# Both expert tables streamed for two latent chunks: scattered and one-hot weights, and a first part of the products kept in DRAM

## The reference

```python
def peer(h, w_q, sub_keys, u_tab, v_tab):
    ...
    def chunk(x):                                      # 128 tokens
        q = (x @ w_q).reshape(PEER_CHUNK, PEER_HEADS, 2, PK_HALF)
        s = jnp.einsum('chpd,hpnd->chpn', q, sub_keys).astype(jnp.float32)
        st, it = lax.top_k(s, PEER_TOPK)
        ...
        best, pos = lax.top_k(cand, PEER_TOPK)
        eidx = jnp.take_along_axis(cidx, pos, axis=-1)  # 8 heads x 16 experts per token
        g = jax.nn.softmax(best, axis=-1)
        act = jax.nn.gelu(jnp.einsum('chkd,cd->chk', u_tab[eidx], x).astype(jnp.float32))
        return jnp.einsum('chk,chkd->cd', (g * act).astype(x.dtype), v_tab[eidx])
```

## Time and profile before

| | us |
|---|---|
| median of 3 runs (2457.07 to 2461.68) | 2457.78 |
| profiled execution, first to last instruction | 2458.3 |
| last score matmul of phase 1 (L986) ends | 1118.95 |
| walk over the `v` table (L1064), first to last | about 1617 to 2065 |

### The profile page before, as it was taken

One profiled execution on the slowest core, in us unless ns is written; L12 is line 12 of the kernel. 1 busy time (PEld: TensorE's weight loads), 2 busy tenths in 40 slices (PEclk: granted clock), 3 DMA queues, 4 the chain that ended last, 5 costly groups with the idle time before them and its releaser, 6 DMA issues.

```text
span 2458.3 us, 20346 instructions
## 1 busy us (share of the span) xinstructions
PE 1778.0 (72%) x6013; PEld 1073.5 (44%) x6013; DVE 1873.6 (76%) x3933; ACT 514.3 (21%) x1283; POOL 1037.4 (42%) x1028
## 2 busy tenths in 40 slices
PE   7799889889887989891334666689999996000185
PEld 3578744444356438451012333556666664000032
DVE  2451588756789466889999999888687987999955
ACT  0563116440024000110004655710000000000111
POOL 0000000115534342443774776334344446777674
PEclk9899999899999999996566877899999998555599
DMA  9785772349955695866998999589999999999997
GB/s 279 250 274 193 233 231 87 113 135 319 353 182 180 215 330 177 288 250 211 384 410 285 390 411 404 200 300 411 414 411 414 411 411 411 410 408 406 364 404 304
DMA packets 296873, 753.43 MB, mean 306 GB/s; under 512 B 21502, under 2 KB 141102, under 8 KB 296244
## 3 DMA queue, kind: packets, MB, share of 16 engines
q0 software_dynamic: 147456, 536.94, 57.3%
q1 hardware_dynamic: 149308, 215.20, 25.0%
HBM read 740.72 MB, written 11.33 MB: 306 GB/s over the span
## 4 chain that ended last, share of the span: by engine, by line
DVE 37%; PE 29%; DMA 16%; POOL 8%; issue 6%; ACT 2%; DVEq 0%; SPq 0%; ACTq 0%; POOLq 0%
PE bank L788 12%; PE pair L788 6%; DVE big L1552 5%; DVE attn L1552 4%; DMA ring_more<-in_peer_u_dram,eidx 4%; DMA attn<-in_peer_u_dram,eidx 4%; DVE work L1552 3%; PE bank L971 3%; POOL work L2118 2%; DVE ring_more L1552 2%; POOL attn L2118 2%; PE bank L761 2%; POOL big L2118 2%; DMA attn<-in_peer_v_dram,eidx 2%; PE bank L1019 1%
## 5 line engine op out<-in xcount | busy, mean ns | idle before, releaser
L1019 PE MATMUL bank<-big,work 128*128 128x512 f32 x176 | 110.6, 767 | 369.4 <-ACT work L1091 266.3
L788 PE MATMUL pair<-big 128*128 128x128 f32 (+1 forms) x1280 | 361.8, 440 | 9.1 <-DVEq L1421 6.2
L2118 POOL DMA_INDIRECT h_all<-in_peer_u_dram,eidx x109 | 122.0, 1119 | 577.9 <-DVEq L1987 352.6
L788 PE MATMUL bank<-big 128*128 128x512 f32 (+1 forms) x1056 | 310.9, 453 | 34.4 <-DVEq L1421 22.7
L1064 PE MATMUL bank<-h_all,big 128*128 128x512 f32 x608 | 266.8, 595 | 4.6 <-DMA h_all<-in_peer_v_dram 4.6
L788 PEld LDWEIGHTS pair<-big 128*128 128x128 f32 x1280 | 197.3, 194 | 160.9 <-issue 158.6
L788 PEld LDWEIGHTS bank<-big 128*128 128x128 f32 x1056 | 169.2, 199 | 172.4 <-issue 165.0
L2118 POOL DMA_INDIRECT attn<-in_peer_u_dram,eidx x166 | 163.1, 983 | 165.5 <-DVE dots L1552 97.9
L1019 PEld LDWEIGHTS bank<-big,work 128*128 128x128 f32 x176 | 38.1, 235 | 427.0 <-issue 394.9
L1552 DVE CUSTOM_DVE_ANT_0 attn<-attn,pair 128x1024 f32<-128x1024 f32 x166 | 199.5, 1219 | 25.3 <-DMA attn<-in_peer_u_dram,eidx 23.0
L1064 PEld LDWEIGHTS bank<-h_all,big 128*128 128x128 f32 x608 | 180.5, 297 | 86.7 <-DMA h_all<-in_peer_v_dram 5.4
(11 more groups left out here) (311 smaller groups left out, 3172.7 us busy)
## 6 DMA issues: line engine op xcount, KB each, us to landing
big<-in_w_in_dram SPq DMA_DIRECT2D x44, 1024.0 KB, 6.5
h_all<-in_peer_v_dram SPq DMA_DIRECT2D x76, 512.0 KB, 6.8
big<-in_w_ada_dram SPq DMA_DIRECT2D x24, 1024.0 KB, 8.1
big<-in_peer_w_q_dram SPq DMA_DIRECT2D x16, 1024.0 KB, 5.6
gf_row<-in_peer_v_dram SPq DMA_DIRECT2D x26, 512.0 KB, 6.8
work<-in_peer_v_dram SPq DMA_DIRECT2D x26, 512.0 KB, 6.8
big<-in_w_rnn_o_dram SPq DMA_DIRECT2D x8, 1024.0 KB, 7.9
big<-in_w_attn_o_dram SPq DMA_DIRECT2D x8, 1024.0 KB, 6.4
```

The costliest lines, as they stand in the source:

```text
L788: last = nc.tensor.matmul(u[:, 0:n], w[:, k, col:col + P], src[:, k, 0:n], start=(k == 0), stop=(k == KD - 1))
L1019: last = nc.tensor.matmul(psum[i][:, :], diag[:, (n - 1) % DIAGS, :], ring[r][:, i * 512:(i + 1) * 512], start=(k == first_by_tensor[c]), ...
L2118: g.indirect_dma_start(dst, None, ins["peer_" + table][0], bass.IndirectOffsetOnAxis(ap=eidx[:, c, k:k + 1], axis=0)).then_inc(landed, 16)
```

## The change

For chunks 1 and 2 the rows of `u` go too. Both tables are streamed, block by block (128 blocks of 128 experts).

- For a block of `u`, PE transposes the tile (`turn_u`, 8 transposes), ACT copies the result (`move_u`), PE multiplies it with the 256 tokens of both chunks (`products`, 8 matmuls of 256 columns), ACT takes the gelu of it (`gelu`).
- The first 34 blocks (`AHEAD_U`) of this are done before any `v` block; their results go to DRAM (`g_later`, 0.131 MB each) and come back. The others run 4 blocks (`LAG`) ahead of the `v` block.
- DVE multiplies the products with the weights of the block (`weigh`, two 128 x 128 operations, one per chunk), and PE multiplies that with the `v` tile (`sums`, four matmuls of 512 columns, as before).
- Chunk 1's weights are scattered by POOL into a matrix in DRAM (`w_flat`, 8.4 MB, 128 indirect DMAs of 128 elements, each adding; `scatter`), which 16 DMAs have filled with zeros early in phase 0. A block of it (0.066 MB) is loaded with each block. Chunk 2's weights are built by one-hots as before (32 builds, now made and scaled on DVE), beside blocks 22 to 32 of `u`; three quarters stay in SBUF.
- Chunk 2's routing moves into and right behind the score loop. Rows are now only those of chunks 0, 3 and 4, all on DVE: 560 behind the loop instead of 772 (of which 100 are multiplied by PE). The ring has 9 buffers: 6 are open first, 8 from turn `C3_ROUTED`, 9 from `C4_ROUTED`.
- DVE's order from there is made by a planner: each row counts 1.3 us, each part of a route 1.8 to 5.3 us, and a `weigh` is put in when the sum reaches its due time (`spent`, `sums_at`). ACT's answers (softmax, gelu of dots, roots) are placed by the same clock (`ask`).
- The loop of phase 1 ends without PE and ACT waiting for DVE.

```diff
-    RING = 29
+    RING = 9
...
+    AHEAD_U, LAG, KEPT, U_BUFS, V_BUFS, W_BUFS, M_BUFS = 34, 4, 8, 2, 4, 3, 2
...
+        return [0, 1, 2, 3, 4, 5] + [6, 7] * (turn >= C3_ROUTED) + [8] * (turn >= C4_ROUTED)
...
+            def turn_u(n):
...
+                for k in range(KD):
+                    last = nc.tensor.transpose(uT_ps(n)[k // 4][:, (k % 4) * P:(k % 4 + 1) * P],
+                                               u_tile[n % U_BUFS][:, k * P:(k + 1) * P], ident[:, :])
...
+            def products(n):
...
+                for k in range(KD):
+                    last = nc.tensor.matmul(a_ps[n % 2], uT_of(n)[:, k, :], featT[:, k, 0:TOKENS], start=(k == 0), stop=(k == KD - 1))
...
+            def sums(n):
+
+                pe.wait_ge(m_ready, n + 1)
+                pe.wait_ge(v_in[n % V_BUFS], 16 * (n // V_BUFS + 1))
...
+            for n in range(AHEAD_U):
+                if n + 1 < AHEAD_U:
+                    turn_u(n + 1)
+                products(n)
+                if n == IDS_AT:
+                    turn_ids()
+                for m in builds_after.get(n, ()):
+                    weights(m)
             for n in range(NKEY):
...
+                if AHEAD_U <= n + LAG < NKEY:
+                    turn_u(n + LAG)
+                sums(n)
+                if AHEAD_U <= n + LAG < NKEY:
+                    products(n + LAG)
...
+            PART_US, ROW_US, HOT_US = (1.8, 1.8, 1.8, 1.8, 4.3, 5.3, 2.8), 1.3, 1.45
+            BOTH_US, SUM_US = 8.2, 3.5
...
+                V.tensor_tensor(m[:, 0:P], g_[:, 0:P], w_first[n % W_BUFS], ALU.mult)
+                V.tensor_tensor(m[:, P:2 * P], g_[:, P:2 * P], w_second[:, n // QI % 3, :, n % QI], ALU.mult).then_inc(m_ready, 1)
...
+            def spent(us):
+
+                clock[0] += us
+                while made[0] < NKEY and clock[0] >= ALONE_US + (WORK - ALONE_US) * sums_at(made[0]) / sums_at(NKEY):
+                    weigh(made[0])
+                    made[0] += 1
...
+            for z in range(ZEROS):
+                g.dma_start(w_zero[z], zero).then_inc(zero_in, 16)
...
+            def scatter(h):
+
+                if h % 2 == 0:
+                    pool.wait_ge(pair_ready, h // 2 + 1)
+                if h:
+                    pool.wait_ge(scattered, 16 * TOPK * h)
+                for k in range(h * TOPK, (h + 1) * TOPK):
+                    g.indirect_dma_start(w_flat, bass.IndirectOffsetOnAxis(ap=widx[:, k:k + 1], axis=0),
+                                         gw[:, C1, k:k + 1], None, compute_op=ALU.add).then_inc(scattered, 16)
...
+            rows(0, BESIDE)
+            pool.wait_ge(zero_in, 16 * ZEROS)
+            for h in range(PH):
+                scatter(h)
+            rows(BESIDE, len(turns))
```

More of the change, by code:

```diff
@@ new lines, in hybrid_step @@
+        w_zero = w_flat.rearrange("(z p x) o -> z p (x o)", p=P, x=D)
+        w_block = w_flat.rearrange("(a p x) o -> a p (x o)", p=P, x=P)
+        g_later = nc.dram_tensor("g_later", (AHEAD_U, P, TOKENS), F32, kind="Internal").ap()
+        w_later = nc.dram_tensor("w_later", (P, QI * P), F32, kind="Internal").ap()
+        zero = h2_all[:, NCH - 1, :]
+        widx = eidx[:, C1, :]
+        tok = sb("tok", [P, 1])
+        iota128 = vcols
+        u_tile, v_tile = [wk(6, 2), wk(8, 2)], [wk(2, 2)] + [h2_all[:, i, :] for i in range(3)]
@@ L715, in _ @@
+            for i in range(1, NCH):
                 store(i)
@@ L1409, in _ @@
+            pe.drain().then_inc(sums_full, 1)
+        asks = {}
         @block.vector
@@ L1711, in topk, with settle @@
                 link(V.max_index(ti[:, 8:16], tv[:, 8:16], cut_))
-            def route(c, pair, between):
-                for i in range(4):
-                    hp = 4 * pair + i
-                    topk(c - C1, hp, late2[:, hp, :] if c == C1 + 1 else late34[:, c - C1 - 2, hp, :])
-                    between(i)
+            def settle(c, pair, between):
                 h = 2 * pair
@@ L1729, in route, with pair_ids, search_second @@
                 between(6)
+            def route(c, pair, between):
+                for i in range(4):
+                    hp = 4 * pair + i
+                    topk(c - C1, hp, late34[:, c - C1 - 2, hp, :])
+                    between(i)
+                settle(c, pair, between)
+            def pair_ids(c, pair):
+                h = 2 * pair
+                places_of_64(c, h)
+                for s in range(2):
+                    expert_side(h, h + 2, s)
+                if c == C1:
+                    pair_places(c, pair)
+            def search_second(hp):
+                u = (1, "sc", hp)
+                dve.wait_ge(bank_free[bank[u]], use[u])
+                topk(1, hp, late2[:, hp, :])
             dve.wait_ge(x_in, 16)
@@ new lines, in spent, with rows_beside, beside, between @@
+            def spent(us):
[3 more added lines that the diff above has]
+                    made[0] += 1
+            def rows_beside(n):
+                for _ in range(n):
+                    rows(1)
+                    spent(ROW_US)
+            def beside(n_rows):
+                def between(i):
+                    spent(PART_US[i])
+                    rows_beside(share(n_rows, i, PARTS))
+                return between
@@ new lines, in _, with hots_beside, between @@
+            next_hot = [0]
+            def hots_beside(pair):
+                def between(i):
+                    spent(PART_US[i])
+                    end = BUILDS * max(PARTS * pair + i - 1, 0) // (2 * PARTS - 2)
+                    for m in range(next_hot[0], end):
+                        one_hots(m)
+                        spent(HOT_US)
+                    next_hot[0] = end
+                return between
+            pair_ids(C1, PAIRS - 1)
+            for pair in range(PAIRS):
+                best_of_64(C1 + 1, 2 * pair)
+                before[0] += 5.0
+                pair_diffs(C1 + 1, pair)
+                pair_ids(C1 + 1, pair)
+                before[0] += 7.0
+                pair_weights(*((C1 + 1, pair - 1) if pair else (C1, PAIRS - 1)))
@@ L2094, in _ @@
+            route(C3, 3, beside(SPREAD))
+            routed(C3)
+            for pair in range(PAIRS):
+                if pair == PAIRS - 1:
+                    dve.wait_ge(final_in, 48)
+                    final(0, wk(4, 2))
+                route(C4, pair, beside(SPREAD // 2))
+            rows_beside(U4 - next_turn[0])
+            dve.wait_ge(row_used, U4)
+            gelu_dots(C3)
             routed(C4)
-            rows(step_start[4] - next_turn[0])
-            step_end(C4)
-            rows(ALONE)
```

1140 lines of the change are left out of this document (541 added, 599 removed).

## The result

The changed kernel takes 2506.6 us (median of 4, 2503.1 to 2508.0), the kernel before beside it 2459.4 us (median of 4): a ratio of 1.0188, 95% interval 1.0173 to 1.0203. It is slower by 47 us where 16 us less was forecast (2442 for 2458). The profiled execution has a span of 2501.3 us, 59 more than the 2442 of the sum.

A forecast was written before the change was run, and what follows sets the result against it. Behind the score loop, mostly DMA megabytes were taken as the bound. PE's stream from 1124, first part to 1325, walk from 1339 to 2393, end at 2412, plus 30 for queues: 2442 us, 8-in-10 range 2398 to 2530.

The forecast's parts named there:

- the scatter: On POOL behind the score loop: 215 us from about 1066, ending near 1280, ahead of the rows, so nothing counted.
- what the walk loses: Queue losses of DMA over the 1054 us walk over v: bounds 18 and 84 us, 30 taken.
- the zeros: Zero fill of 8.4 MB ahead of phase 1: bounds 0 and 20 us, 5 taken.
- three signs of being wrong: Long stretch's DMA rate under 390 GB/s, PE waiting for tiles, or the walk starting later than 1355.
- What is to be had: Behind the score loop: 452 MB for 498, the 46 MB less worth 112 us at 411 GB/s.
- The score loop: DVE falls some 13 us behind PE but catches up; PE starts on the u stream at 1124.
- The first 34 blocks: PE's u blocks at 4.33 us each, 148 us with the first turn, plus 53 for builds, ending at 1325.
- the rival of a slow PE: First 34 blocks of u at 1.2 GHz: 148 + 34 us more, about 2620; chance 0.03.
- the rival of the late scatter: From 1.6 us per scatter, rows and w_flat blocks wait; at 2.0 us each, 2488 in all; chance 0.12.
- The walk: Walk over v from 1339, longest engine sum per stretch: 136, 187, 677 and 54, together 1054 us, before queue losses.
- The last eight blocks: Blocks 120 to 127: 16 us of rows, 9 of chunk 4's sums and norm, 29 of PE: 54 us.
- The queues lose 8%: Six buffers and three engines near their limit in blocks 32 to 55 cost 84 us: 2496; chance 0.22.

The follow-up runs named there:

- the four edits: Changed kernel with zeros spread, last weigh earlier, ACT's answers one block earlier, and six gathers ahead of the scatter with small blocks ahead of V tiles 1 to 3: 2439.4 us.
- ask_early: Changed kernel with ACT answering DVE's five late requests one block of u earlier: 2489.7 us.
- combo_beside: The four edits together, with 44 instead of 32 rows used inside the score loop: 2458.5 us.
- before_again: The kernel before, unedited, run again to have its profile from the same set: 2537.1 us.

## Why the prediction was wrong, step by step

Faster was forecast, and it came out slower. The step that failed is the one that counted nothing for the scatter: the way from the last one-hots to the first `weigh` took 23 us more than the sum had. Two more terms were of the right kind and too small: what the walk loses (64 us for 30) and the zeros (13 for 5). Of the three signs of being wrong that were set, one came: the walk starts at 1365, later than 1355. The long stretch ran at 397 GB/s on average and not under 390, and PE never waited for a tile in it.

**The bytes: right.** 453 MB behind the score loop for 452, and a full rate of 404 to 411 behind 1620 against 399 to 407 now. "What is to be had" stands as a sum of bytes (45 MB, 110 us for 112); with the four edits the kernel ends up 21 us under the kernel before.

**The zeros: taken as 5 us within 0 to 20, measured 13.** The step read that there was room in DMA's share at 150 to 200 us. But the zeros go at 56 to 64, in one burst of 8.4 MB, and PE's tiles had to share the DMA engines with it (410 GB/s from 64 to 72 us, while PE waited). The window to read was that one. Spread out, they cost nothing that can be seen.

**The score loop: right**, pace and hand-over, but for 3.2 us at the hand-over.

**The first 34 blocks: right.** 4.33 us a block, and the whole stretch with its builds 194 us for 201. PE's clock is at 0.98 to 1.00 (the level of 2.4 GHz) from 1124 to 1300 with 8 transposes among 24 records, so the rival of a slow PE is out. The Trainium skill, "TensorE: Matmul & The Clock Gate", "Part 4: PE-mode transpose", says that transposes don't count as busy in the same way; the trace shows the clock at full speed in this mix all the same. DMA moved 119 to 129 GB/s up to 1300 for 140.

**The scatter: this step failed.** It took 1.24 us each, from a gather, and "so I count nothing". A scatter takes 1.55 us on POOL with 0.30 to the next, and 17 us went for landings, 265 us in all for the 215 of the sum: the rival of the late scatter, whose decision point was 1.6 us each. It also began 14 us late (1079.8 for 1066), when POOL had waited 20 us for DVE; so it ended at 1344.5, 64 us behind the 1280 of the sum. POOL's row of this run gives what it should have been:

```profile
L2206 POOL DMA_INDIRECT w_flat<-gw,eidx x128: 1537/1545/2269, 1079.8 to 1342.9; - x128
```

The price of the gather was read as the whole distance between two, 0.94 and 0.30 us, and taken as the lower bound for the scatter; then the forecast stood on that bound, although 7 us stood at the other end. The sentence on read-modify-write below 512 B in the Trainium skill, "DMA: Bandwidth & Descriptors", "Specifications", had spoken for more; that this is where the 0.6 us come from is not shown by any run. The lateness cost DVE 19 us, but the run without scatter got back only 9: the other half of the term is the wait for a small block that stands behind the scatter, issued at the same moment as V tiles and nine rows, which the sum had at nothing.

**The walk: +34 of 1084, at the sizes of three terms.** By stretches: blocks 0 to 31 took 152 for 136, 32 to 55 209 for 187, 56 to 119 698 for 677, and 120 to 127 59 for 54; so 64 us where 30 were laid aside. The bounds of 18 and 84 held it. The prediction put these losses down to the ring, and the runs show another cause for much of them: 17 us (or more) go with two waits for an answer of ACT, which one line takes away. The prediction knew of seven such waits and left them "within these bounds". The ring was not what lost most of it in the long stretch: with nine buffers DMA is full there (share 1.01), and three buffers fewer cost 21 in the whole. Whether more than six would have helped in the first 144 rows, no run tells.

In the first blocks there is a wait that neither the sum nor an edit took up. DVE waits 19 us for blocks of `g_later`, all of it by 1518, where 16 us were lost against the sum (DVE's waits in the walk: in all, times, longest):

```profile
DVE ktok L1761 <- DMA work<-g_later: 13.0, 7, 6.7
...
DVE attn L1761 <- DMA work<-g_later: 6.3, 5, 2.5
```

Meanwhile DMA moved 388 GB/s up to 1480 and 361 behind it, which against 411 is some 11 us lost by 1518; how much of that is this wait, no run tells.

**The last eight blocks: sized right, read wrong.** 54 was forecast and 59 measured. The order itself leaves DMA at 72 GB/s there, and a constant of the planner gives back 29 us; the prediction took the order for given. As a term of the sum it did no harm.

**The rivals.** *The scatter is late* came true, with 23 us for 46 at 2.0 us each (by its own ends, 1378 against the 1325 at which rows are wanted, that was 53). *The queues lose 8%* came true in size (6.1% of 1054) and in a part of its mechanism: blocks 32 to 55, where it had three engines near their limit, lost 22 us, 12 of which earlier answers of ACT give back (197 us in ask_early for 209). A single one of them would have left the change at 2465 or 2476, near the 2458 of before. It was their sum with the zeros, so the error was also one of weighing: three costs were each set near their lower end. The measured time lies inside the range of 2398 to 2530, and "slower" had a chance of 0.44; the likeliest case had the sign wrong.

**Why the change loses 47 us though it moves 54 MB less.** Of the 54 MB, 45 are saved where it counts, behind the score loop, and worth 110 us at 411 GB/s. Against that stands the time in which DMA is not full. From 1119 us to its end the kernel before needs 1339 us for 498 MB, which are 1212 at 411: 127 lost. The changed kernel needs 1377 (1124 to 2501) for 453 MB, which are 1102: 275 lost, 160 of it in the first part alone (33 MB, 81 us of full rate, in 241 us), 115 in the walk and the tail. 148 more lost against 110 saved are 38 us, and the cut at 1124 for 1119 adds 5: that is the 43 between the two spans. The edits show that 67 us of the 275 and of what comes ahead were no property of the idea but of four places in the order. That the 160 are the idea's own price is argued, not shown: PE, DVE and POOL are each busy for 74 to 79 per cent of these 241 us (PE for 92 per cent up to 1300), and the one edit that moved rows (combo_beside) made the start of the walk 25 us later for 5 us behind it.

## What to carry to other kernels

A saving in bytes is worth its time only where DMA is full; add up separately the stretches that the change leaves DMA idle, and look at the window in which each new transfer really goes, not at a neighbour with room. Where a fixed order joins several engines, list every wait for another engine's answer at its place in the order and price it as a block, and look for who is left working when the bound resource has finished. An operation that no trace shows should not be booked at the price of its nearest relative without asking what hangs on its end.

## What the runs showed of the hardware

**A scatter of single elements with an add, 128 to an instruction:** 1.55 us on POOL against 0.94 for a gather of 128 rows of 4 KB, and 2.4 us of POOL's time at each wait for the landing of 16 (16.6 us for seven such waits).

**Gathers are slower on POOL in the changed kernel when DMA is full.** From 1960 to 2200 us the same instruction has (groups: busy, mean ns), first in the changed kernel, then in the kernel before:

```profile
L2167 POOL DMA_INDIRECT attn<-in_peer_u_dram,eidx x18 | 23.9, 1328 | 7.8 <-issue 4.6 <-DVE dots L1239 2.3 <-DVE big L1251 0.9
```

```profile
L2118 POOL DMA_INDIRECT attn<-in_peer_u_dram,eidx x24 | 25.9, 1081 | 9.1 <-issue 4.6 <-DVE dots L1552 4.5
```

In both stretches DMA is full (406 and 410 GB/s), so that alone isn't it; the changed kernel has more transfers from SP (25 MB for 16) and `w_flat` blocks of 512 B packets beside. No cost of it is visible here, as DMA was the bound. The cause is open; no run was made for it.

**The kernel before has a second level, 3% up, in some sets of runs.** There is one profile of it. In before_again DVE stands still in the middle of one topk, between operations that wait for no other engine. DVE's timeline there, then the same operations in the first profile:

```profile
1213.13 0.09 DVE L1707 MATCH_VALUE_LOAD big<-big 128x8 f32 x1 [9.53 <-issue]
...
1218.73 0.29 DVE L1710 MAX8 big<-work 128x8 f32<-128x128 f32 x1 [4.99 <-remote]
```

```profile
1201.00 0.09 DVE L1707 MATCH_VALUE_LOAD big<-big 128x8 f32 x1
...
1201.64 0.29 DVE L1710 MAX8 big<-work 128x8 f32<-128x128 f32 x1
```

DMA stands at a share of 1.03 up to 1213 and 1.02 from there to 1221, and drops to 0.28 only behind the standstill (1221 to 1226): there the low rate follows DVE's pause and doesn't cause it. Waits of DVE that nothing in the trace ends come to 27 us from 1200 to 1500, and to none in the kernel before at its faster level. What DVE waited for is open: the trace names no releaser, and no run was made for it. The effect of this level on the study: the ratio of one pair of kernels went from 1.0188 to 0.9919 between sets, and a comparison across sets is good to some 8 us for the changed kernel and not at all for the kernel before.
